# A fused two-block transformer kernel: the low parts of the weights in four instructions instead of one, and the forget bias as one float32r matmul

## What is computed

```
log_f = log_sigmoid(f_logit)                      # (S, 8 heads)
c = cumsum(log_f, axis=1)
s = q_i @ k.T * scale + (c[query] - c[key])       # per head
p = softmax(where(key <= query, s, -inf))
out = p @ v
```

## Time and profile before

| what | us |
|---|---|
| median of three executions | 3812.3 |
| lowest and highest of them | 3809.74 and 3812.32 |
| the profiled execution | 3810.42 |
| its span | 3808.7 |
| TensorE matmul busy in it | 3564.5 (94%) |
| VectorE busy | 1734.1 (46%) |
| GpSimd busy | 1388.5 (36%) |
| ScalarE busy | 1290.1 (34%) |

### The profile page before, as it was taken

The page is one execution under the profiler, slowest core; times in us unless marked ns, Lnnn a source line. Parts: engine busy times, 40 slices in busy tenths (PEclk is TensorE's granted clock), DMA queues, the critical chain, the costliest instruction groups (busy, mean ns, idle before and its releaser), DMA issues.

```text
span 3808.7 us, 46006 instructions
## 1 busy us (share of the span) xinstructions
PE 3564.5 (94%) x15608; PEld 2826.5 (74%) x15608; DVE 1734.1 (46%) x2305; ACT 1290.1 (34%) x1751; POOL 1388.5 (36%) x617
## 2 busy tenths in 40 slices
PE   5958799999998999989999999989999899999999
PEld 4836666678887887767777788778877677777887
DVE  4955655466564335641333433443346413334334
ACT  3334344332223222563452322232225534522221
POOL 3412222334443444333224444434443332244443
PEclk9979899999999999999999999999999999999999
DMA  5211134222232222122112222222221221122222
GB/s 189 94 39 45 45 122 144 99 83 94 94 102 86 94 99 94 67 78 84 60 61 89 89 97 96 106 78 98 95 94 67 78 89 56 61 93 85 99 94 105
DMA packets 90997, 337.10 MB, mean 89 GB/s; under 512 B 10096, under 2 KB 10480, under 8 KB 90224
## 3 DMA queue, kind: packets, MB, share of 16 engines
q1 hardware_dynamic: 85392, 313.68, 23.5%
q10 hardware_dynamic: 5472, 21.65, 1.7%
HBM read 333.19 MB, written 2.10 MB: 88 GB/s over the span
## 4 chain that ended last, share of the span: by engine, by line
issue 59%; PE 20%; POOL 19%; POOLq 1%; DVE 0%; ACT 0%; DVEq 0%; ACTq 0%
POOL w_lo L420 19%; PE ps L428 6%; PE ps L430 6%; PE ps L429 6%; PE ps L793 1%; PE ps L811 0%; PE ps L791 0%; PE ps L560 0%; PE ps L561 0%; PE ps L562 0%; PE ps L802 0%; POOLq L417 0%; PE ps L517 0%; POOLq L419 0%; POOLq L420 0%
## 5 line engine op out<-in xcount | busy, mean ns | idle before, releaser
L420 POOL TENSOR_TENSOR w_lo<-raw,w_hi 128x1024 fp32r<-128x1024 f32 x570 | 1378.3, 2420 | 2398.3 <-ACT w_hi L890 2398.2
L428 PE MATMUL ps<-a_hi,w_lo 128*128 128x512 f32 x3056 | 1221.8, 400 | 68.9 <-DVE a_lo L1414 32.3
L430 PE MATMUL ps<-a_hi,w_hi 128*128 128x512 f32 x3056 | 1198.9, 392 | 0.0
L429 PE MATMUL ps<-a_lo,w_hi 128*128 128x512 f32 x3056 | 1198.9, 392 | 0.0
L890 ACT ACTIVATE w_hi<-raw 128x1024 fp32r<-128x1024 f32 x572 | 602.6, 1056 | 1129.7 <-PE ps L430 1103.1
L428 PEld LDWEIGHTS ps<-a_hi,w_lo 128*128 128x128 f32 x3056 | 580.1, 190 | 213.9 <-issue 42.7
L430 PEld LDWEIGHTS ps<-a_hi,w_hi 128*128 128x128 f32 x3056 | 579.0, 189 | 123.5
L429 PEld LDWEIGHTS ps<-a_lo,w_hi 128*128 128x128 f32 x3056 | 579.9, 190 | 121.5 <-issue 4.5
L428 PE MATMUL ps<-b_hi,w_lo 128*128 128x512 f32 x1312 | 514.5, 392 | 3.8 <-DVE xres L1719 3.6
L429 PE MATMUL ps<-b_lo,w_hi 128*128 128x512 f32 x1312 | 511.1, 390 | 0.0
L430 PE MATMUL ps<-b_hi,w_hi 128*128 128x512 f32 x1312 | 511.0, 390 | 0.0
(11 more groups left out here) (218 smaller groups left out, 2703.5 us busy)
## 6 DMA issues: line engine op xcount, KB each, us to landing
raw<-in_stream SPq DMA_DIRECT2D x573, 512.0 KB, 3.2
arena<-in_mod_w ACTq DMA_DIRECT2D x32, 512.0 KB, 3.6
arena<-in_mod_w SPq DMA_DIRECT2D x16, 512.0 KB, 8.4
xres<-in_x_t SPq DMA_DIRECT2D x1, 2048.0 KB, 8.3
xres<-in_x_t ACTq DMA_DIRECT2D x1, 2048.0 KB, 8.0
arena<-in_lru ACTq DMA_DIRECT2D x2, 1024.0 KB, 6.1
out_t<-xres SPq DMA_DIRECT2D x1, 2048.0 KB, 6.3
arena<-in_c_row SPq DMA_DIRECT2D x1, 512.0 KB, 9.7
```

Source lines behind the costliest of these rows:

```text
L420: pool.tensor_tensor(w_lo[:, s, :], raw[:, s, :], w_hi[:, s, :].bitcast(F32), ALU.subtract).then_inc(lo_ready, 1)
L428: pe.matmul(out, lo, x_hi, start=start, stop=False)
L429: pe.matmul(out, hi, x_lo, start=False, stop=False)
L430: return pe.matmul(out, hi, x_hi, start=False, stop=stop)
```

## The change

GpSimd's one 128x1024 subtraction becomes four of 128x256, of which the last raises `lo_ready`.

The forget logits are projected to two groups of rows, 0 to 7 and 32 to 39 (the weights and the bias are laid out twice on the host), so that the chain on VectorE and ScalarE works on 40 partitions. Behind the scan VectorE rounds the sum to float32r in `cum_split` and, on rows 32 to 39, puts the remainder in its place. `pick` has for each head a one in row h and in row 32 + h. The bias is then one float32r matmul over 128 partitions, rounded part and remainder in one.

```diff
+LOW = 32
+F_ROWS = LOW + HEADS
+        cum_split = sb("cum_split", [P, S], F32R)
+        pick = sb("pick", [P, HEADS], F32R)
-        neg_cum_f = row_tile[0:HEADS, :]
-        f_row, f_abs = tt[0:HEADS, 0, :], tt[0:HEADS, 1, :]
+        neg_cum_f = row_tile[0:F_ROWS, :]
+        f_row, f_abs = tt[0:F_ROWS, 0, :], tt[0:F_ROWS, 1, :]
@@ gpsimd
-                    pool.tensor_tensor(w_lo[:, s, :], raw[:, s, :], w_hi[:, s, :].bitcast(F32), ALU.subtract).then_inc(lo_ready, 1)
+                    for q in range(4):
+                        part = slice(q * 2 * P, (q + 1) * 2 * P)
+                        last = pool.tensor_tensor(w_lo[:, s, part], raw[:, s, part], w_hi[:, s, part].bitcast(F32), ALU.subtract)
+                    last.then_inc(lo_ready, 1)
@@ tensor, attend
-                    pe.matmul(ps[:, 4 + c.sc.n % 2, w], ident[0:HEADS, h:h + 1].to_broadcast([HEADS, P]), neg_cum_f[:, w],
+                    pe.matmul(ps[:, 4 + c.sc.n % 2, w], pick[:, h:h + 1].to_broadcast([P, P]), cum_split[:, w],
                               start=False, stop=True).then_inc(scores_done, 1)
@@ vector, before the first norm
+            dve.memset(cum_split[:, :].bitcast(F32), 0.0)
+            dve.tensor_tensor(pick[:, :], ident[:, 0:HEADS], ident[:, LOW:LOW + HEADS], ALU.add)
@@ vector, the forget chain of each layer
-                        dve.tensor_tensor_scan(neg_cum_f, ones[0:HEADS, :], f_row, 0.0, ALU.mult, ALU.add).then_inc(cum_ready, 1)
+                        dve.tensor_tensor_scan(neg_cum_f, ones[0:F_ROWS, :], f_row, 0.0, ALU.mult, ALU.add)
+                        dve.drain()
+                        dve.tensor_copy(cum_split[0:F_ROWS, :], neg_cum_f)
+                        dve.drain()
+                        low = cum_split[LOW:F_ROWS, :]
+                        dve.tensor_tensor(low, row_tile[LOW:F_ROWS, :], low.bitcast(F32), ALU.subtract).then_inc(cum_ready, 1)
@@ host
-        forget = np.concatenate([w[:, 3 * D:at], np.zeros((D, P - HEADS), np.float32)], axis=1)
+        forget = np.zeros((D, P), np.float32)
+        forget[:, 0:HEADS] = forget[:, LOW:LOW + HEADS] = w[:, 3 * D:at]
```

More of the change, by code:

```diff
@@ L1349, in _ @@
                         act.drain()
-                        act.activation(f_abs, f_abs, ACT.Ln, bias=one_col[0:HEADS, :]).then_inc(f_logged, 1)
+                        act.activation(f_abs, f_abs, ACT.Ln, bias=one_col[0:F_ROWS, :]).then_inc(f_logged, 1)
                         c.op.n += 2 * KT
@@ L1903, in _ @@
                         dve.wait_ge(tiles_done, c.tiles.at(0))
-                        dve.tensor_scalar(f_row, ps[0:HEADS, 4, :], par(PAR2, "b_f")[0:HEADS, :], None, ALU.add).then_inc(f_asked, 1)
+                        dve.tensor_scalar(f_row, ps[0:F_ROWS, 4, :], par(PAR2, "b_f")[0:F_ROWS, :], None, ALU.add).then_inc(f_asked, 1)
                         dve.wait_ge(f_logged, c.cum.at(1))
@@ L2028 @@
         b_f = np.zeros((P, 1), np.float32)
-        b_f[0:HEADS, 0] = b[3 * D:at]
+        b_f[0:HEADS, 0] = b_f[LOW:LOW + HEADS, 0] = b[3 * D:at]
         par2.append(np.concatenate([
```

## The result

| | kernel before | kernel after |
|---|---|---|
| median, us | 3811.0 (3809.5 to 3812.3, 4 runs) | 3746.3 (3741.3 to 3747.7, 4 runs) |
| span of the profiled execution, us | 3808.7 | 3744.9 |

The ratio is 0.9828, with a 95% interval of 0.9811 to 0.9845. The direction was right, the size half of what came.

The account below looks back on a forecast made before the run. TensorE was taken to bound the attention, VectorE or GpSimd a few other places. Bias -42.6, chain +0.6, first uses +2, recurrences +10, convolution 0 and start -2 gave -32 us: 3778 us, range 3756 to 3795.

Parts of the forecast that it names:

- The bias matmul: Attention, where TensorE is the bound: one float32r matmul over full rows saves 2.66 us per set of four, 42.6 us.
- the surcharge: Attention: the bias matmul over 8 rows costs 0.09 us ahead of it and 0.19 us in it, because of the rows.
- The third: Bias matmul in attention: float32r over a spread-out column runs in four passes, 30 us more, 3808 us; chance 0.04.
- the fourth rival: Attention: steps wait for VectorE's maximum and ScalarE's exponential, half the gain is lost, +21 us, 3799 us; chance 0.05.
- The chain that feeds it: VectorE's added work ahead of `conv4`, at most 1.5 us per layer, costs 0; additions before the first norm cost +0.6 us.
- The start: Start: two tiny VectorE instructions wait about 0.6 us each, 3.0 us earlier; a slowed second unit leaves -2 us.
- Recurrences: Six `recurrence` places between projections: units in quarters reach TensorE later, 1.7 us each, +10 us (bounds 0 and +29).
- First uses: Eight places outside the recurrences where TensorE waits for `w_lo`: 0.25 us more each, +2 us (0 to 7).
- The convolution: Convolution, 18 units: four quarters hold VectorE as long as one whole, 0, with 9 us either way.
- second rival: Turns favour VectorE more than they cost TensorE: recurrences 0, convolution -9 us, 3760 us; chance 0.13.
- the slower rival: Convolution, HGRN heads and recurrences: each turn at the shared port costs extra, 3834 us with 0.25 us each; chance 0.05.
- The fifth rival: Shared port: each quarter holds VectorE longer by t, 120 turns; no gain from t = 0.05 us; chance 0.05.

Follow-up runs that it names:

- e1: The kernel after, but GpSimd forms each unit's low part in one instruction as before: 3765.1 us, ratio 0.9881.
- e5: The kernel before, but its float32 bias matmul works over all 128 rows instead of 8: 3791.3 us, ratio 0.9951.
- e11: The kernel after, but with one GpSimd instruction per unit in the two stretches of recurrences only: 3733.9 us, ratio 0.9798.
- e6: The kernel after, but its float32r bias matmul works over the 40 rows that hold data instead of 128: 3767.0 us, ratio 0.9884.

## Why the prediction was off

**The bias matmul: right.** Forecast 42.6 us. By the pairs above, 128 columns save 0.43 us and 512 save 0.91, so four widths on the line between save 2 x 1.34 = 2.68 us and 16 sets 42.9. All 64 pairs together hold TensorE for 87.2 us before and 43.8 after, 43.4 less. The attention stages show 43.4 us, with the 1.1 us ahead of each 45.6, and e1 44.4. That the pairs and the stages agree is in part chance: the kernel after and e1 lose 1.6 us in each stage to the clock, and without that the stages give more than the pairs. Some of it is in the transposes L802 behind the pairs, 1.4 us in each layer. Reading the surcharge from the next row's start was right too, and e5 shows that it goes with the rows. The price of 128 columns in float32r was near its lower bound: 0.29 us for the pair, less 0.22 for L798 (0.86 / 4), is 0.07 us, not 0.12. The third and the fourth rival are gone with it: L800 is one pass, and the waits of TensorE in the attention are as few as before.

**The chain that feeds it: right.** The stage ahead of the recurrences is unchanged within 0.1 us.

**The start: the small instructions as forecast, the gain smaller.** L1485 and L1489 take 0.52 and 0.58 us. The stage gives 1.1 us where the sum has -2 + 0.6 = -1.4.

**Recurrences: right.** +10 forecast, +9.2 measured, and e11 gives it back. The mechanism was only partly mine. I had both units of a `recurrence` late by about 2 us. The trace has the first one late by that, and the second hardly. And 1.2 us of each stage are TensorE's lower clock, for which I had no term, so the size came out partly by luck.

**First uses: too high by little.** Leaving out the one long wait before the first projection, TensorE waits for low parts 14.2 us at L435 and 8.5 us at L567, against 7.2 and 5.7 us before. These are the lines for the whole kernel after:

```profile
PE ps L435 <- POOL w_lo L426: 35.7, 12, 21.5
PE ps L567 <- POOL w_lo L426: 8.5, 4, 4.6
```

That is 9.8 us more, and 7.2 of it are in the two recurrence stages. So 2.6 us are left for all other places, against my 2 us. The one of 21.5 us is no new wait: in the kernel before the same idle time was put down to VectorE, and the start became shorter.

**The convolution: the step that failed.** I wrote that four quarters hold VectorE as long as one whole: 0, with 9 us each way. It was -7.4 us. The numbers for the better value stood in my own text: a unit of 2.4 us held VectorE for 2.2, so a part of each GpSimd instruction doesn't hold VectorE. By the experiments that part is about 0.28 us whatever the width. With four instructions there are four such stretches, and a unit takes 1.67 us from VectorE instead of 2.13. The sign that I had named, rounds of about 4.9 us where a unit falls in, is absent too: they are 3.90 and 4.58 us. I took the fixed part only as something that lengthens GpSimd, and not as something that VectorE can use. This was my second rival's half of -9 us, which I had tied to another mechanism and given 0.13.

**HGRN heads and feed-forward: steps that were missing.** I named the HGRN heads only within the slower rival, as a place where turns could cost. They gave 9.8 us, about half by shorter waits and half by the higher clock that came with them. The feed-forward of the first block I took for a stretch that TensorE bounds, since it is busy there for 345.99 of 360.00 us. But the 14 us of pauses are enough for 8.9 us. L1733 with its mean of 2596 ns, against about 0.7 for an instruction of its size, was the row to see.

Together the three give 26.1 us. With 45.6 - 42.6 = 3.0 us for the bias, 0.8 for the recurrences and -0.3 for the start, the difference comes to 29.6 of the 31.8 us between my sum and the spans. The rest is about my allowance of 2 us for first uses, whose waits lie within the stages that are counted already. The fifth rival, a price t for each turn, has the opposite sign: t is about -0.1 us ((1.67 - 2.13) / 4). Beside this, my 3778 us is for the profiled execution; for the median I should have added its 1.9 us.

**What stays open.** The 0.28 us are worked out from VectorE's counts and GpSimd's times; no run shows what GpSimd does in them, or where in the instruction they lie. That the clock in the HGRN heads rises because the waits are shorter fits every run, but no experiment changed the clock alone. Why it falls behind the same wait of 3.1 us in the attention of some kernels and not of others isn't known.

## What to carry to other kernels

When two engines exclude each other at a port, ask for each stage which engine is late, and how long the single hold is as well as the sum: look for instructions whose mean is a multiple of what their size takes, and for what is queued behind them. Splitting the intruder helps where the other engine sets the pace and costs where the intruder's own result is awaited, so choose the split by stage. A small matmul that accumulates onto a big one should have all of its rows, padded with zeros where need be. And read the granted clock of a stage before you explain a difference of one or two microseconds in it.

## What the hardware showed that I had not expected

- A matmul over 8 or 40 rows next to ones over 128 costs about 0.1 us ahead of it and 0.2 us in it, in float32 and in float32r: 19.7 us for 64 of them in e5, 20.6 us in e6. Its weight load takes no longer, but starts with its matmul and not 0.43 us ahead.
- VectorE loses less to a GpSimd unit the more instructions it is cut into, 2.13, 1.97, 1.67 and 1.20 us: about 0.28 us of each instruction cost it nothing. Meanwhile GpSimd's busy time for low parts grows, from 1378.3 us with whole units to 1758.0 with quarters.
- With eight parts GpSimd hardly rests from 99 to 192 us (92.8 of 93 us), though each instruction moves only 128 columns; half of their mean of 914 ns is waiting for VectorE, since most of them over the whole kernel take 460 ns.
- Waits of TensorE that become shorter can give back its clock as well: in the HGRN heads the mean granted clock is 0.90 with whole units and 0.92 to 0.94 with split ones, and the same matmuls take 5.0 us less in the kernel after.
